# Expert weights issued by two engines in whole loads, and first-block scores from split halves

## The reference, cut to what matters

```python
# first block: 8 query heads of 64 with 2 key heads (global), and 8 with 8 (dilated windows)
qa = apply_axial_rope(rms_norm(qa, qa_norm_g), tables)
ka = apply_axial_rope(rms_norm(ka, ka_norm_g), tables)
sc = jnp.einsum('bqkgd,bskd->bkgqs', qb, k, preferred_element_type=jnp.float32) * scale
p = jax.nn.softmax(sc, axis=-1)
...
# second block: top-1 group, top-2 of its 8 experts; 32 experts in all
def expert_block(args):
    xb, e = args
    return (jax.nn.silu(xb @ w_gate[e]) * (xb @ w_up[e])) @ w_down[e]
```

## Time and profile before

| | us |
|---|---|
| median of 3 runs (all: 1490.48, 1491.85, 1496.7) | 1491.85 |
| the profiled execution | 1495.09 |
| its span, first to last instruction | 1493.3 |
| PE busy in it | 1427.6 (96%) |
| DVE busy | 892.2 (60%) |
| ACT busy | 541.8 (36%) |
| TensorE clock granted, mean | 0.993 |
| moved by DMA | 312.58 MB |

### The profile page before, as it was taken

How to read it: one execution, slowest core, us unless ns; L and a number is a source line. 1 busy time by engine, 2 the same in 40 slices (tenths; PEclk the granted TensorE clock), 3 DMA queues, 4 the chain that set the end, 5 groups by cost and what they waited for, 6 DMA issues and landing times.

```text
span 1493.3 us, 20216 instructions
## 1 busy us (share of the span) xinstructions
PE 1427.6 (96%) x7800; PEld 985.5 (66%) x7800; DVE 892.2 (60%) x1672; ACT 541.8 (36%) x990; POOL 80.1 (5%) x118
## 2 busy tenths in 40 slices
PE   9999999999999999999999898989999999899996
PEld 8786667888888888888887777773344344433432
DVE  4856884558777668774574786463444444444445
ACT  5555774543353332263334885321111111110112
POOL 0001000000000000001001432000000000000000
PEclk9999999999999999999999999999999999999998
DMA  7313010354553348732012013379999999999992
GB/s 254 104 57 128 2 58 1 105 178 129 142 153 113 111 149 283 251 106 92 29 58 99 30 43 121 151 306 362 422 424 421 424 422 422 422 423 421 423 421 118
DMA packets 113483, 312.58 MB, mean 209 GB/s; under 512 B 13887, under 2 KB 65503, under 8 KB 91883
## 3 DMA queue, kind: packets, MB, share of 16 engines
q1 hardware_dynamic: 110131, 303.30, 53.7%
q0 software_dynamic: 2944, 7.87, 1.5%
q10 hardware_dynamic: 312, 0.10, 0.0%
HBM read 311.18 MB, written 4.25 MB: 211 GB/s over the span
## 4 chain that ended last, share of the span: by engine, by line
PE 85%; ACT 5%; DVE 4%; issue 3%; SPq 2%; DMA 1%; POOL 0%; DVEq 0%; POOLq 0%; ACTq 0%
PE bank L1529 79%; PE bank L1532 7%; ACT hTc L1492 1%; SPq L951 1%; ACT hT_high L1183 0%; ACT arena L1443 0%; SPq L948 0%; ACT ring L1412 0%; DVE ring L2512 0%; DVE weights_low L2130 0%; DMA xn<-normed_tokens,token_index 0%; DVE arena L2561 0%; ACT weights_high L1112 0%; DVE x_res L2589 0%; ACT hTc L1160 0%
## 5 line engine op out<-in xcount | busy, mean ns | idle before, releaser
L1529 PE MATMUL bank<-weights_high,hT_high 128*128 128x512 f32 (+2 forms) x672 | 235.0, 384 | 5.7 <-DVE hT_low L2176 3.8
L1529 PE MATMUL bank<-weights_low,hT_high 128*128 128x512 f32 (+2 forms) x528 | 199.7, 378 | 0.0
L2130 DVE TENSOR_TENSOR weights_low<-ring,weights_high 128x2048 fp32r<-128x2048 f32 (+2 forms) x59 | 131.1, 2221 | 107.9 <-ACT weights_high L1112 107.0
L1529 PE MATMUL bank<-hT_high,weights_high 128*128 128x512 f32 (+1 forms) x448 | 170.0, 379 | 1.5 <-DVE hT_low L2176 1.5
L1529 PE MATMUL bank<-hT_high,weights_low 128*128 128x512 f32 (+1 forms) x448 | 167.6, 374 | 0.0
L1529 PE MATMUL bank<-hT_low,weights_high 128*128 128x512 f32 (+1 forms) x448 | 167.6, 374 | 0.0
L1112 ACT ACTIVATE weights_high<-ring 128x2048 fp32r<-128x2048 f32 (+2 forms) x59 | 109.5, 1855 | 156.6 <-PE bank L1529 146.7
L1529 PEld LDWEIGHTS bank<-weights_high,hT_high 128*128 128x128 f32 x672 | 126.7, 189 | 30.1 <-issue 6.7
L1529 PEld LDWEIGHTS bank<-weights_low,hT_high 128*128 128x128 f32 x528 | 99.7, 189 | 17.8 <-issue 0.2
L1529 PEld LDWEIGHTS bank<-hT_high,weights_high 128*128 128x128 f32 x448 | 84.3, 188 | 20.2 <-issue 4.0
L1529 PEld LDWEIGHTS bank<-hT_high,weights_low 128*128 128x128 f32 x448 | 84.3, 188 | 15.1
(11 more groups left out here) (365 smaller groups left out, 2563.8 us busy)
## 6 DMA issues: line engine op xcount, KB each, us to landing
arena<-in_w_down SPq DMA_DIRECT2D x16, 2048.0 KB, 25.6
ring<-in_w_down SPq DMA_DIRECT2D x16, 2048.0 KB
xn<-in_w_ada SPq DMA_DIRECT2D x48, 512.0 KB, 4.7
ring<-in_w_up SPq DMA_DIRECT2D x44, 512.0 KB, 5.3
arena<-in_w_gate SPq DMA_DIRECT2D x22, 1024.0 KB, 24.9
arena<-in_w_up SPq DMA_DIRECT2D x22, 1024.0 KB, 25.4
ring<-in_w_gate SPq DMA_DIRECT2D x22, 1024.0 KB, 24.9
ring<-in_w_up SPq DMA_DIRECT2D x22, 1024.0 KB, 26.0
```

The lines of the kernel that those rows point to most:

```text
L1529: return nc.tensor.matmul(o, lhsT, rhs, start=start, stop=stop)
L2130: low_ready.tick(v.tensor_tensor(part_view(w_low, key), raw_view(key), part_view(w_high, key), ALU.subtract), k)
```

## The change

It has two parts that don't touch each other.

**Scores from split halves.** ACT's copies of the transposed queries and keys now write high parts; DVE gets sixteen new steps `qk_low(m)`, which subtract them from the bank to make the low parts; they free the bank (`qk_split`) in the place of the copies. DVE does `qk_low(n - 3)` at the head of pass n of its loop. PE makes each pair of scores as three products of either member, alternating between the two.

**Expert loads by two engines.** SP issues only gate and up: of experts 3 to 29 as whole loads of 2 MB each after `gu_filled`, of experts 0, 1, 2, 30 and 31 by halves as before. Down of expert n+2 is issued by ACT, between `expert(n)` and `result_high(n)`, with the same wait; that of expert 31 in two halves with a semaphore each.

```diff
-                banks.plan(("qkT", n), (qk_drained, n))
+                banks.plan(("qkT", n), (qk_split, n))
...
             for n in range(E - 2):
-                if n + WAYS < E:
+                if n + WAYS in IN_ROWS_OF_HALVES:
                     load_gate_and_up(sp, n + WAYS, n % WAYS, n + 1)
-                load_down(sp, n + 2, n % 2, n + 1)
+                elif n + WAYS < E:
+                    load_whole(sp, n + WAYS, n % WAYS, n + 1)
...
+        def load_whole(sp, e, place, reuse):
+
+            sp.wait_ge(gu_filled, reuse)
+            for i, name in enumerate(("w_gate_2", "w_up_2")):
+                sp.dma_start(GATE_UP[place][i], inp[name].rearrange("a e (p j) f -> (a e) p (j f)", j=KT)[e]).then_inc(
+                    first_in[place], 16)
...
-                        ins = s.activation(qaT[:, :, at], b3, ACT.Copy)
+                        ins = s.activation(qa_high[:, :, at], b3, ACT.Copy)
...
                 expert(n, n % 2, n - 1 if n >= 2 else None)
+                if n + 2 < E:
+                    load_down(act, n + 2, n % 2, n + 1)
                 result_high(n, n % 4, (n // 2 - 1) * TT if n >= 4 else None)
...
-            qk_drained.wait(pe, 15)
+            qk_split.wait(pe, 15)
...
-                        ql, k = (qbT[half, h // 2, at], kB[half, h // 2, :]) if m else (qaT[half, h % 4, at], kA[half, :])
-                        banks.close(mm(bank[:, :], ql, k, True, True), ("score", i))
+                        sides_of.append(pairs(*queries, *held_keys))
+                    for n in range(3):
+                        for bank, i in zip(into, (2 * q, 2 * q + 1)):
+                            last = mm(bank[:, :], *sides_of[i % 2][n], n == 0, n == 2)
...
-                        for i in range(2):
-                            pe.wait_ge((first_in, second_in)[j // 4][2 * place + i], held(pe, 16 * loads + 16))
+                    if j == 0:
+                        pe.wait_ge(first_in[place], held(pe, 32 * loads + 32))
+                    if j == 4 and halved is not None:
+                        pe.wait_ge(second_in[place], held(pe, 32 * halved + 32))
...
+            def qk_low(m):
+
+                c, t = PROJ[m]
+                b3 = banks.filled(dve, ("qkT", m))[:, :].rearrange("p (j n) -> p j n", j=4)
+                qk_drained.wait(dve, m)
...
+                        ins = v.tensor_tensor(low[:, into:into + b - a, at], b3[:, a:b, :], high[:, into:into + b - a, at],
+                                              ALU.subtract)
+                qk_split.tick(ins, m)
+
             for n in range(20):
                 if n - 1 in HIGH_AFTER:
                     low_part("w_in", HIGH_AFTER[n - 1])
+                if n >= 3 and n - 3 < 16:
+                    qk_low(n - 3)
```

More of the change, by code:

```diff
@@ L285, in two_blocks @@
         assert DIST_AT == TT * 640 + 5 * 512 + 10 * T + 8 * T
+        QK_AT = TT * 640 + 5 * 512
+        qa_high, qb_high, kA_high, kB_high = (over(name, shape, arena_at + 4 * (QK_AT + at)) for name, shape, at in (
+            ("qa_high", [P, 4, T], 0), ("qb_high", [P, 4, T], 4 * T), ("ka_high", [P, T], 8 * T), ("kb_high", [P, 4, T], 9 * T)))
+        qa_low = over("qa_low", [P, TT, D], xn_at)[:, :, 512:1024]
+        qb_low, kB_low = over("qb_low", [P, 4, T], early_at), over("kb_low", [P, 4, T], early_at + 4 * 4 * T)
+        kA_low = over("ka_low", [P, T], arena_at + 4 * (DIST_AT - T))
         junk1, rope_t = carve(0, D, of=spare), carve(D, 2, 512, of=spare)
@@ L404, in two_blocks @@
         qk_ready = steps("qk_normed", range(16))
-        qk_drained = steps("qk_transposed", range(16))
+        qk_drained = steps("qk_high_parts", range(16))
+        qk_split = steps("qk_low_parts", range(16))
         NU = 2 * H * TT
@@ L763, in two_blocks, with halved_ahead @@
         WAYS = len(GATE_UP)
+        IN_ROWS_OF_HALVES = [n for n in range(E) if n < WAYS or n >= E - 2]
+        def halved_ahead(n):
+            return len([m for m in IN_ROWS_OF_HALVES if m < n and m % WAYS == n % WAYS])
         final_gain = carve(0, D, of=xn[:, 0:1, :].rearrange("p a n -> p (a n)"))
@@ L766, in two_blocks @@
         normed_out = carve(0, TT, D)
-        first_in = [sem(f"expert_first_rows_in{i}") for i in range(2 * WAYS)]
-        second_in = [sem(f"expert_second_rows_in{i}") for i in range(2 * WAYS)]
+        first_in = [sem(f"expert_first_rows_in{i}") for i in range(WAYS)]
+        second_in = [sem(f"expert_second_rows_in{i}") for i in range(WAYS)]
+        last_down_in = sem("last_down_rows_in")
         down_in = [sem("expert_down_in0"), sem("expert_down_in1")]
@@ L867, in load_rows @@
             at = slice(half * 4 * EF, (half + 1) * 4 * EF)
-            sp.dma_start(GATE_UP[place][i][:, at], rows[:, at]).then_inc((first_in, second_in)[half][2 * place + i], 16)
+            sp.dma_start(GATE_UP[place][i][:, at], rows[:, at]).then_inc((first_in, second_in)[half][place], 16)
         def load_down(sp, e, par, reuse):
@@ L873, in load_down @@
                 sp.wait_ge(y_filled, reuse)
-            sp.dma_start(DOWN[par], inp["w_down_2"].rearrange("a e (p f) d -> (a e) p (f d)", f=4)[e]).then_inc(
-                down_in[par], 16)
+            rows = inp["w_down_2"].rearrange("a e (p f) d -> (a e) p (f d)", f=4)[e]
+            if isinstance(e, int) and e == E - 1:
+                sp.dma_start(DOWN[par][:, 0:2 * D], rows[:, 0:2 * D]).then_inc(down_in[par], 16)
+                sp.dma_start(DOWN[par][:, 2 * D:4 * D], rows[:, 2 * D:4 * D]).then_inc(last_down_in, 16)
+            else:
+                sp.dma_start(DOWN[par], rows).then_inc(down_in[par], 16)
         def load_gate_and_up(sp, e, place, reuse):
@@ L1648, in _ @@
                 if q < NP:
+                    into = [banks.open(pe, ("score", i)) for i in (2 * q, 2 * q + 1)]
+                    sides_of = []
                     for i in (2 * q, 2 * q + 1):
                         m, h, t = unit_of(i)
-                        bank = banks.open(pe, ("score", i))
                         half, at = slice(HD * (i % 2), HD * (i % 2) + HD), slice(t * P, t * P + P)
-                        ql, k = (qbT[half, h // 2, at], kB[half, h // 2, :]) if m else (qaT[half, h % 4, at], kA[half, :])
-                        banks.close(mm(bank[:, :], ql, k, True, True), ("score", i))
+                        queries = [part[half, h // 2 if m else h % 4, at] for part in ((qb_high, qb_low) if m else (qa_high, qa_low))]
+                        held_keys = [part[half, h // 2, :] for part in (kB_high, kB_low)] if m else [
+                            part[half, :] for part in (kA_high, kA_low)]
+                        sides_of.append(pairs(*queries, *held_keys))
+                    for n in range(3):
+                        for bank, i in zip(into, (2 * q, 2 * q + 1)):
+                            last = mm(bank[:, :], *sides_of[i % 2][n], n == 0, n == 2)
+                            if n == 2:
+                                banks.close(last, ("score", i))
                 if 1 <= q <= NP:
@@ L2008, in tokens_in_place, with gate_and_up @@
                 last.then_inc(xt_filled, 1)
-            def gate_and_up(m, par, place, loads):
+            def gate_and_up(m, par, place, loads, halved):
                 tokens = xT[m % 2 if isinstance(m, int) else 0]
@@ L2039, in down @@
                 for f in range(4):
+                    if isinstance(n, int) and n == E - 1 and f == 2:
+                        pe.wait_ge(last_down_in, 16)
                     for half in range(2):
@@ L2082, in _ @@
                     pair_piece(pair, t)
-                gate_and_up(n // 2, n % 2, n % WAYS, n // WAYS)
+                gate_and_up(n // 2, n % 2, n % WAYS, n // WAYS, halved_ahead(n) if n in IN_ROWS_OF_HALVES else None)
                 if n + 2 < E:
@@ L2223, in _ @@
                 link(v.tensor_scalar(head_gain[:, n, :], head_gain[:, n, :], -HD ** -0.5, None, ALU.mult))
+            def qk_low(m):
+                c, t = PROJ[m]
+                b3 = banks.filled(dve, ("qkT", m))[:, :].rearrange("p (j n) -> p j n", j=4)
+                qk_drained.wait(dve, m)
+                at = slice(t * P, t * P + P)
+                parts = {0: [(qa_low, qa_high, 0, 4, 0)], 1: [(kA_low, kA_high, 0, 1, 0), (qb_low, qb_high, 2, 4, 0)],
+                         2: [(qb_low, qb_high, 0, 2, 2), (kB_low, kB_high, 2, 4, 0)], 3: [(kB_low, kB_high, 0, 2, 2)]}[c]
+                for low, high, a, b, into in parts:
+                    if low is kA_low:
+                        ins = v.tensor_tensor(low[:, at], b3[:, 0, :], high[:, at], ALU.subtract)
+                    else:
+                        ins = v.tensor_tensor(low[:, into:into + b - a, at], b3[:, a:b, :], high[:, into:into + b - a, at],
+                                              ALU.subtract)
+                qk_split.tick(ins, m)
             for n in range(20):
```

10 lines of the change are left out of this document (5 added, 5 removed).

## The result

The changed kernel takes 1518.75 us (median of 4 runs, 1511.28 to 1523.68) against 1491.16 for the kernel before on the same chip: ratio 1.017, 95% interval 1.0142 to 1.0198. The forecast was 1486.3, with 1481 to 1496 as its range; rival 2 said 1519. The profiled execution of the changed kernel is its fastest, 1511.28 us with a span of 1509.4.

What follows compares the result with a forecast made beforehand. PE was taken to bound projection and first attention, DMA the later expert stage. Scores and low parts -3.9, whole loads -1.6, down on ACT 0: -5.5 us from the median 1491.85 gives 1486.3, range 1481 to 1496.

Steps and rivals of the forecast that it cites:

- rival 2: Expert stage: token gather, sharing with a third queue and larger rows, lands 3.8 us late per pair; +27 us, 1519; chance 0.17.
- What bounds the kernel: PE bounds projection and first attention; in the experts DMA is full throughout, PE equally at first, then DMA sets the pace.
- The scores: First attention: a pair of scores takes 0.89 us instead of 1.06, saving 5.4 us over 32 passes; bounds 0 and 11.8.
- The low parts: Projection: DVE's added subtractions make PE wait once for a bank near 66.6 us, costing 1.5 us; bounds 0 and 3.
- Whole loads: Expert stage: a later DMA start costs 3.4 us, larger rows save 5.0; sum -1.6 us, from -6 to +3.4.
- The term of 3.4: Start of expert stage: expert 3's gate load waits until 1014.40 instead of 1010.96, moving the end by +3.4 us.
- Down on ACT: Expert stage: issuing down from ACT changes only the issuer; loads still land 25 us after issue; costed at 0.
- the order of issue: Assumption that SP's and ACT's loads are served as issued, read from a 4 KB load that took 5.4 us.
- rival 1: Expert stage: down on ACT's queue overtakes gate and up, so PE's waits for down go; -2.4 us, 1483.9; chance 0.15.

Runs made afterwards that it cites:

- down by SP: The changed kernel with down issued by SP again instead of ACT, whole gate and up loads kept: 1487.98 us, ratio 0.9968 to the kernel before.
- scores alone: The kernel before with only the split scores and low parts added, every expert load by SP and by halves as before: 1489.62 us, ratio 0.9976.
- two token buffers: The changed kernel with a second buffer for gathered tokens, so each gather is issued a pair of experts ahead: 1485.85 us, ratio 0.9956 to the kernel before.

## Why the prediction was wrong, point by point

**What bounds the kernel.** Right. DMA and PE were both at their limit, and the kernels with less than 3 us of waits for the gather all lie at 420 to 427 GB/s (1041 to 1440 us) and at ratios of 0.9947 to 0.9976, whatever else they change.

**The scores: 5.4 us.** Right. A pair now takes 179.75 - 178.85 = 0.90 us, forecast 0.89. A whole pass went from 3.36 to 3.20 us in the chain, 32 x 0.16 = 5.1 us:

```profile
178.85 0.50 PE L1557 MATMUL bank<-kb_high,qb_high 64*128 64x512 f32 x2
179.19 0.40 PE L1557 MATMUL bank<-kb_low,qb_high 64*128 64x512 f32 x2
179.42 0.40 PE L1557 MATMUL bank<-kb_high,qb_low 64*128 64x512 f32 x2
179.75 0.44 PE L1560 MATMUL bank<-const,arena 128*128 128x128 f32 x2
```

**The low parts: one wait of 1.5 us in the projection.** Right, at the place that was named. PE's waits from 40 to 122 us:

```profile
PE bank L1557 <- ACT arena L1247: 1.3, 1, 1.3
```

The range of these two parts was too narrow by their own bounds, which give -11.8 to +3 and not -10 to +1. It didn't matter here.

**Whole loads: +3.4 and -5.0.** The sign and the size of the rate are right: 427 and 426 GB/s with down by SP against 422, by which 27 experts of 6.29 MB take 4 to 5 us less. Whole loads against halves, both by SP, are 0.9968 against 0.9976, -1.2 us where -1.6 was forecast, which is within the noise of both. The term of 3.4 is not confirmed. Wrong was that the row size had only these two effects: on a queue beside ACT's, it also sets how long the gather's packets wait.

**Down on ACT: costed at 0.** This is the step that failed: the term was put at nothing, and PE lost 38.1 us in 13 waits for the gather in place of 18.0 for down. With whole loads in place, this step alone is 0.9968 to 1.017, some 30 us. It rested on "the chip serves the two in the order of issue", read from one load of 4 KB that took 5.4 us; by it down should have landed 25 us after issue, and it landed after 14.2. That row was as good for turns as for order, and another row in the same group of arguments spoke openly for turns: the gather landed in 9.6 us on POOL's queue while SP's loads took 25.6. I named it in favour of rival 1 and gave it too little weight.

**Rival 1.** Its mechanism is there: with halves and down on ACT, down lands in 11.6 us and the waits for it are gone. Its price isn't shown: 0.9961 against 0.9976 for the scores alone would be -2.2 us, but the intervals overlap, and the waits went over to up (16.1 us for down became 13.4 for up). That gate and up had time in hand was wrong; with DMA full somebody has to wait.

**Rival 2.** Right in kind and place: the gather late in 13 pairs. That its sum is met too, 1519 against 1518.75, is luck, for its parts were wrong. The lateness is 38.1/13 = 2.9 us a pair, not 3.8; against this stands the clock, which no term had, 8.7 us in the profiled execution. The two profiled spans lie only 16.1 us apart (1509.4 and 1493.3), the medians 27.6. The spread of the other runs goes with their clock, though without traces of them it isn't shown whether longer waits came with it: they took 1516.04, 1523.68 and 1521.46 at mean granted clocks of 0.985, 0.981 and 0.984, against 1511.28 at 0.989; if a thousandth of clock is a thousandth of the span, 1.5 us (an estimate), this gives 6, 12 and 8 for measured differences of 4.8, 12.4 and 10.2. And the cause wasn't a third queue with large rows at all times, but that the gather's last packets run into the next down. That the next down is issued 4 us after the gather, within its 11.0 us, stood in the trace before; I didn't lay the two beside each other.

## What to carry to other kernels

A load that moves to another engine's queue changes no bytes but changes who stands behind whom: for every small transfer with a deadline, write down its window (here 11.0 us) and its landing time (9.6 to 11.1), and treat a margin of nothing as the first thing that breaks. Row size is part of the order of service, since queues take turns by rows: larger rows gained 1% in rate, and the gather landed in 10.7 in place of 10.0 us beside SP's queue alone, in 13.8 in place of 9.0 beside both. Where two edits share one slack, test them together, not only one by one. The new scores alone were 0.24% faster than the kernel before, with either load edit added 0.3 to 0.4%, with both 1.7% slower, and a second buffer for the late transfer turned that into 0.44% faster.

## What the runs showed of the hardware

- Down on a queue of its own lands in 14.3 us (two token buffers), on the shared one in 25.7 (down by SP), at the same total rate of 426 GB/s.
- A gather lands in 10.7 us beside SP's rows of 16 KB, in 11.2 with a down on a second queue beside its first 7 us, and in 13.8 with one beside its last part.
- On its own queue down lands in 11.6 us beside rows of 8 KB and in 14.2 beside rows of 16 KB.
- The sustained rate with SP's queue alone was 422 GB/s with rows of 8 and 16 KB mixed, 426 to 427 with rows of 16 KB.
- A load of 4 KB took 1.7 us with only ACT's load of 65 KB beside it, and 5.4 beside SP's first loads too.
- Of 13 waits of PE of 1.7 to 3.8 us, 6 were followed by a stretch that took 1.3 to 1.6 us longer than elsewhere, with 0.57 to 0.71 of the clock granted in its first 4 us. Their length alone doesn't tell which: behind 2.29 us it came, behind 3.27 it didn't.
